# Last projection of a hybrid encoder layer: gate products one step ahead, and the merge's loads issued inside it

## The reference, cut to what matters

```python
xn = _rmsnorm(x, norm1_g)
z = xn @ w_in
u_x, u_g, q, k, v, f_logit, g_rnn, g_attn = jnp.split(z, SPLIT_POINTS, axis=-1)
...
rnn_y = (jax.nn.gelu(u_g) * h_seq.astype(x.dtype)) @ w_rnn_out
...
attn_y = attn.reshape(B, T, D_ATTN) @ w_attn_out
x = x + (jax.nn.sigmoid(g_rnn) * rnn_y + jax.nn.sigmoid(g_attn) * attn_y) @ w_o
x = x + _hier_moe(_rmsnorm(x, norm2_g), w_route_group, b_route_group, ...)
```

## Time and profile before

| | before |
|---|---|
| median of 3 runs | 2563.87 us |
| the profiled execution | 2562.86 us |
| its span | 2560.9 us |
| TensorE busy | 2178.7 us (85%) |
| VectorE busy | 1346.7 us (53%) |
| ScalarE busy | 1138.2 us (44%) |
| granted TensorE clock, mean | 0.932 |

### The profile page before, as it was taken

How to read it: one execution, slowest core, us unless ns; L and a number is a source line. 1 busy time by engine, 2 the same in 40 slices (tenths; PEclk the granted TensorE clock), 3 DMA queues, 4 the chain that set the end, 5 groups by cost and what they waited for, 6 DMA issues and landing times. The chain is left out here.

```text
span 2560.9 us, 36881 instructions
## 1 busy us (share of the span) xinstructions
PE 2178.7 (85%) x11116; PEld 1764.8 (69%) x11116; DVE 1346.7 (53%) x1576; ACT 1138.2 (44%) x1545; POOL 231.8 (9%) x299
## 2 busy tenths in 40 slices
PE   4469897988889897699999978995957999999993
PEld 2357675766767674599988868994845777777772
DVE  5423645455363545511155553213256888888886
ACT  3223444434344443321166543112224777777772
POOL 0210202112020200000000000000000100101013
PEclk9779999999999997799999998997978999999996
DMA  3310302111130201211122223104036999999997
GB/s 91 69 34 10 86 20 65 33 52 51 35 85 9 60 25 35 104 48 43 50 79 88 90 69 120 46 28 163 34 125 237 392 398 393 398 393 397 394 392 256
DMA packets 199087, 351.65 MB, mean 137 GB/s; under 512 B 19764, under 2 KB 127464, under 8 KB 198936
## 3 DMA queue, kind: packets, MB, share of 16 engines
q1 hardware_dynamic: 181560, 293.55, 32.1%
q0 software_dynamic: 13872, 44.74, 5.7%
q10 hardware_dynamic: 3584, 12.58, 1.2%
HBM read 301.87 MB, written 48.97 MB: 137 GB/s over the span
## 5 line engine op out<-in xcount | busy, mean ns | idle before, releaser
L2312 DVE TENSOR_TENSOR e_w_lo<-e_raw,e_w_hi 128x2048 fp32r<-128x2048 f32 x189 | 427.6, 2290 | 83.6 <-ACT e_w_hi L2242 65.2
L2242 ACT CAST e_w_hi<-e_raw 128x2048 fp32r<-128x2048 f32 x189 | 360.6, 1910 | 51.5 <-PE e_y_ps L103 33.7
L101 PE MATMUL proj_ps<-w_qkv_hi,xh 128*128 128x384 f32 x544 | 233.4, 429 | 24.8 <-PEq L287 19.1
L101 PE MATMUL ux_ps<-xh,r_wx_hi 128*128 128x364 f32 x576 | 191.4, 332 | 19.0 <-DVE r_wx_lo L768 15.5
L102 PE MATMUL ux_ps<-xl,r_wx_hi 128*128 128x364 f32 x576 | 190.5, 331 | 0.0
L103 PE MATMUL ux_ps<-xh,r_wx_lo 128*128 128x364 f32 x576 | 190.3, 330 | 0.0
L103 PE MATMUL proj_ps<-w_qkv_hi,xl 128*128 128x384 f32 x544 | 188.6, 347 | 0.0
L102 PE MATMUL proj_ps<-w_qkv_lo,xh 128*128 128x384 f32 x544 | 188.5, 346 | 0.0
L1188 PE MATMUL out_ps<-mT 128*128 128x512 f32 (+3 forms) x384 | 171.0, 528 | 2.9 <-DVEq L84 2.3
L101 PEld LDWEIGHTS proj_ps<-w_qkv_hi,xh 128*128 128x128 f32 x544 | 107.0, 197 | 51.3 <-issue 45.1
L1387 ACT ACTIVATE mT<-st_ps 128x512 f32<-128x512 f32 x192 | 93.9, 489 | 104.4 <-PE st_ps L1173 49.6
(11 more groups left out here) (425 smaller groups left out, 5107.9 us busy)
## 6 DMA issues: line engine op xcount, KB each, us to landing
e_raw<-w_gate_e SPq DMA_DIRECT2D x64, 1024.0 KB, 8.1
e_raw<-w_up_e SPq DMA_DIRECT2D x64, 1024.0 KB, 8.7
e_raw<-w_down_e SPq DMA_DIRECT2D x64, 1024.0 KB, 8.0
w_raw<-w_in SPq DMA_DIRECT2D x24, 512.0 KB, 4.4
r_wx<-w_in SPq DMA_DIRECT2D x24, 512.0 KB, 3.7
slot_y<-e_y ACTq DMA_DIRECT2D x32, 384.0 KB, 6.1
slot_y<-zrows POOLq DMA_DIRECT2D x24, 368.0 KB, 4.4
mT<-cache_k SPq DMA_DIRECT2D x8, 1024.0 KB, 5.5
```

The costliest lines, as they stand in the source:

```text
L101: nc.tensor.matmul(out, a_hi, b_hi, start=start, stop=False)
L2242: sc.copy(w_hi[u][:, :], w.raw[c][:, :]).then_inc(wh_ready, 1)
L2312: v.tensor_tensor(w_lo[u][:, :], w.raw[c][:, :], w_hi[u][:, :], ALU.subtract).then_inc(wl_ready, 1)
```

## The change

It has four parts.

1. `recurrent` ends with three steps more: SyncE loads the weights of gate 1, ScalarE takes gate 0's sigmoid (into a new tile `gate_sig` with two slots) and casts the weights, VectorE subtracts.
2. The last projection is a function of its own, `project_last`. TensorE's order is gate 1, projection 0, gate 2, projection 1, ..., gate 7, projection 6, projection 7. The sigmoid of gate c+1 goes to the slot that projection c doesn't use. Weights still pass through the one buffer `r_wx`, in the order projection 0, gate 2, projection 1, gate 3, ...
3. `w_o` is loaded as a whole, in four DMAs of 1 MB, over `xl`, and x over `xh`, as soon as gate 7's product has ended, by SyncE inside the projection's block. `merge` then casts and subtracts from there.
4. `turned_sb` of the merge has buffers of its own, and `got` of the expert stage lies over `mT`.

```diff
--- before.py
+++ after.py
@@ -455,6 +455,8 @@
                     load_bd(c + 1)
                 sp.wait_ge(x_split, KT)
                 sp.dma_start(w_x[:, :, :], g.w_in_k[:, :, COL_GATE_RNN:COL_GATE_RNN + P]).then_inc(g.gate_loaded, 16)
+                sp.wait_ge(g.gate_split, KT + 1)
+                sp.dma_start(w_x[:, :, :], g.w_in_k[:, :, COL_GATE_RNN + P:COL_GATE_RNN + 2 * P]).then_inc(g.gate_loaded, 16)
                 sp.wait_ge(tails_kept, 1)
...
@@ -571,6 +573,11 @@
                 with act.Fori(0, KT - 1) as c:
                     step(c, True)
                 step(KT - 1, False)
+                act.wait_ge(g.gate_ready, KT + 1)
+                nc.scalar.activation(g.sig[:, 0, :].rearrange("p (j t) -> p j t", t=THIRD), ux_ps[:, :, 0:THIRD], ACT.Sigmoid)\
+                    .then_inc(g.sig_ready, 1)
+                act.wait_ge(g.gate_loaded, KT * 16 + 32)
+                nc.scalar.copy(wx_split[0][:, :, :], w_x[:, :, :]).then_inc(g.gate_rounded, 1)
...
@@ -637,6 +644,8 @@
                     step(c, True)
                 step(KT - 1, False)
                 dve.sem_inc(tails_ready, 1)
+                dve.wait_ge(g.gate_rounded, KT + 2)
+                v.tensor_tensor(wx_split[1][:, :, :], w_x[:, :, :], wx_split[0][:, :, :], ALU.subtract).then_inc(g.gate_split, 1)
                 dve.wait_ge(tails_turned, 1)
                 edge(v.tensor_copy(tails_T[0:(2 * H + 2) * KT, :], ug_ps[0:(2 * H + 2) * KT, 0, 0:P]), tails_kept)
...
+def project_last(nc, g, sems, branch, w_out, gate_col):
...
+                load_p(0)
+                for k in range(KT):
+                    sp.dma_start(b_raw[:, k, :], branch[k]).then_inc(b_loaded[load_of(k)], 16)
+                with sp.Fori(0, KT - 2) as c:
+                    sp.wait_ge(p_split, before + c + 1)
+                    alone(sp, g)
+                    load_g(c + 2)
+                    sp.wait_ge(g_split, before + c + 3)
+                    alone(sp, g)
+                    load_p(c + 1)
+                sp.wait_ge(p_split, before + KT - 1)
+                load_p(KT - 1)
+                sp.wait_ge(gate_ready, before + KT)
+                for n in range(W_O_LOADS):
+                    ks = slice(n * KT // W_O_LOADS, (n + 1) * KT // W_O_LOADS)
+                    sp.dma_start(g.xn2[:, ks, :], g.w_o[0].rearrange("(k p) n -> p k n", p=P)[:, ks, :]).then_inc(g.wo_loaded[n], 16)
+                sp.dma_start(g.x1[:, 0:PT, :], g.x_prompt[0].rearrange("(t p) n -> p t n", p=P)).then_inc(g.x1_loaded, 16)
+                sp.dma_start(g.x1[0:T_SAMPLE, PT, :], g.x_sample[0]).then_inc(g.x1_loaded, 16)
...
+                with pe.Fori(0, KT - 1) as c:
+                    gate(c + 1)
+                    proj(c)
+                proj(KT - 1)
...
+                def squash(c, odd):
+                    act.wait_ge(gate_ready, before + c + 1)
+                    act.wait_ge(proj_taken, before + c)
+                    nc.scalar.activation(thirds(sig[:, odd, :]), gate_ps[:, :, 0:THIRD], ACT.Sigmoid).then_inc(sig_ready, 1)
+
+                def step(c, odd, more=True):
+                    act.wait_ge(proj_ready, before + c)
+                    round_p(c)
+                    squash(c + 1, 1 - odd)
+                    if more:
+                        round_g(c + 2)
+
+                squash(1, 1)
+                round_g(2)
+                with act.Fori(0, 2) as i:
+                    step(i * 2 + 1, 1)
+                    step(i * 2 + 2, 0)
+                step(5, 1)
+                step(6, 0, False)
+                act.wait_ge(proj_ready, before + KT - 1)
+                round_p(KT - 1)
...
+                def join(c, odd):
+                    chain = Chain(dve, chain_v, before + c * V_STEPS)
+                    dve.wait_ge(proj_ready, before + c + 1)
+                    dve.wait_ge(sig_ready, before + c + 2)
+                    m = g.mT[:, bass.ds(c, 1), 0:T_WIDE].rearrange("p o t -> p (o t)")
+                    chain(v.tensor_tensor(thirds(sig[:, odd, :]), thirds(sig[:, odd, :]), proj_ps[:, :, 0:THIRD], ALU.mult))
+                    chain(v.tensor_tensor(m, m, sig[:, odd, :], ALU.add), proj_taken)
+                    chain.ended(V_STEPS)
+
+                def step(c, odd, more=True):
+                    join(c - 1, 1 - odd)
+                    rest_p(c)
+                    if more:
+                        rest_g(c + 2)
+
...
+                rest_g(2)
+                with dve.Fori(0, 2) as i:
+                    step(i * 2 + 1, 1)
+                    step(i * 2 + 2, 0)
+                step(5, 1)
+                step(6, 0, False)
+                step(7, 1, False)
+                join(7, 1)
...
-        W_PARTS, K_EACH = KT, 1
-        w_raw = [sb(f"w_raw{b}", [P, K_EACH, D]) for b in range(2)]
+        w_raw = xn2
...
-        turned_sb = [raw[:, 0, :].rearrange("p (k t) -> p k t", k=KT) for raw in w_raw]
+        turned_sb = [sb(f"turned{b}", [P, KT, P]) for b in range(2)]
...
-                load_w(0)
-                load_w(1)
-                sp.dma_start(x1[:, 0:PT, :], g.x_prompt[0].rearrange("(t p) n -> p t n", p=P)).then_inc(x_loaded, 16)
-                sp.dma_start(x1[0:T_SAMPLE, PT, :], g.x_sample[0]).then_inc(x_loaded, 16)
...
-                for n in range(2, W_PARTS):
-                    sp.wait_ge(w_split, n - 1)
-                    load_w(n)
...
-                for n in range(W_PARTS):
-                    act.wait_ge(w_loaded[n % 2], 16 * (n // 2 + 1))
-                    sc.copy(w_o[0][:, ks_of(n), :], w_raw[n % 2][:, :, :]).then_inc(w_rounded, 1)
+                for k in range(KT):
+                    act.wait_ge(g.wo_loaded[k * W_O_LOADS // KT], 16)
+                    sc.copy(w_o[0][:, k, :], w_raw[:, k, :]).then_inc(w_rounded, 1)
...
-                for n in range(W_PARTS):
-                    dve.wait_ge(w_rounded, n + 1)
-                    v.tensor_tensor(w_o[1][:, ks_of(n), :], w_raw[n % 2][:, :, :], w_o[0][:, ks_of(n), :], ALU.subtract).then_inc(w_split, 1)
+                for k in range(KT):
+                    dve.wait_ge(w_rounded, k + 1)
+                    v.tensor_tensor(w_o[1][:, k, :], w_raw[:, k, :], w_o[0][:, k, :], ALU.subtract).then_inc(w_split, 1)
-                dve.wait_ge(x_loaded, 32)
+                dve.wait_ge(g.x1_loaded, 32)
...
-        got = [sb(f"got{t}", [P, D]) for t in range(NT)]
+        got_all = g.mT[:, :, :].rearrange("p k t -> p (k t)").rearrange("p (t n) -> p t n", n=D)
+        got = [got_all[:, t, :] for t in range(NT)]
...
-            with nc.sbuf_tensor("xn2", [P, NT, D], F32) as xn2:
-                merge(nc, g, x1, xn2, logits, tables)
...
+    g.mT = ctx.enter_context(nc.sbuf_tensor("mT", [P, KT, T_PAD], F32, side="right"))
+    rest = ExitStack()
+    g.xh = sb("xh", [P, KT, T_PAD], F32R)
+    x_end = nc.sbuf_base
+    g.xl = rest.enter_context(nc.sbuf_tensor("xl", [P, KT, T_PAD], F32R))
+    rest_end = nc.sbuf_base
+    assert KT * T_PAD == NT * D
+    g.x1, g.xn2 = (nc.alloc_sbuf_tensor_at(name, [P, NT, D], F32, offset=end - NT * D * 4) for name, end in (("x1", x_end), ("xn2", rest_end)))
+    g.wo_loaded, g.x1_loaded = [g.sem(f"wo_loaded{n}") for n in range(W_O_LOADS)], g.sem("x1_loaded")
...
-        project(nc, g, sems, 1, g.y_T, g.w_rnn_out, COL_GATE_RNN, True, "pr")
+        project_last(nc, g, sems, g.y_T, g.w_rnn_out, COL_GATE_RNN)
```

More of the change, by code:

```diff
@@ L2365, in _, with back @@
                                                x1[0:rows(t), t, :], ALU.mult, ALU.add).then_inc(summed, 1)
[L2368 removed]
+def back(nc, g, rest):
     with ExitStack() as ctx:
[L2371 to L2372 removed]
+        sb = lambda name, shape, dt=F32: ctx.enter_context(nc.sbuf_tensor(name, shape, dt, side="right"))
         gates, slots = sb("gates", [P, TOP_K, NT]), sb("slots", [P, TOP_K, NT], U32)
@@ L2375, in back @@
         tokens = sb("tokens", [CAP, BLOCKS_MAX + 2], U32)
-        with nc.sbuf_tensor("logits", [P, NT, GROUPS + EXPERTS], F32) as logits, ExitStack() as kept:
-            tables = RouteTables(nc, kept)
-            with nc.sbuf_tensor("xn2", [P, NT, D], F32) as xn2:
-                merge(nc, g, x1, xn2, logits, tables)
-            mixed.close()
-            with ExitStack() as weights:
-                w = ExpertWeights(nc, g, weights)
-                s = ExpertParts(nc, g, weights)
-                route(nc, g, w, s, tables, logits, gates, slots, passes, expert_of, tokens)
-                experts(nc, g, w, s, passes, expert_of, tokens, x1, gates, slots)
+        logits = sb("logits", [P, NT, GROUPS + EXPERTS])
+        tables = RouteTables(nc, ctx)
+        merge(nc, g, g.x1, g.xn2, logits, tables)
+        rest.close()
+        w = ExpertWeights(nc, g, ctx)
+        s = ExpertParts(nc, g, ctx)
+        route(nc, g, w, s, tables, logits, gates, slots, passes, expert_of, tokens)
+        experts(nc, g, w, s, passes, expert_of, tokens, g.x1, gates, slots)
```

(6 more changed lines are left out.)

102 lines of the change are left out of this document (82 added, 20 removed).

## The result

| | before | changed |
|---|---|---|
| median | 2562.94 us (4 runs, 2557.91 to 2565.27) | 2537.9 us (4 runs, 2537.37 to 2540.69) |
| the profiled execution | 2562.86 us | 2537.56 us |
| its span | 2560.9 us | 2535.7 us |
| granted clock, mean | 0.932 | 0.936 |

The ratio is 0.9902, 95% interval 0.9888 to 0.9915: 1.0% faster, inside the range and 1.6 us from the forecast. Of the 25.3 us between the two profiled executions I forecast 24.3. That the sum came so near is partly luck: it was 2.6 us short at the first edge and 1.0 at the second, and a loss of 2.6 us behind them made up for most of it.

What follows compares the result with a forecast made beforehand. The DMA-bound expert stage (635 us) stays untouched; idle TensorE edges at the last projection and merge can give time. Gains 2.2 + 22.1 = 24.3 us off the 2563.87 median give 2539.6, forecast 2539.5, range 2533 to 2547.

Steps and rivals of the forecast that it cites:

- first edge: Start of the last projection, where TensorE stood still 17.09 us: putting gate 1's product first gains 2.2 us.
- second edge: Start of the merge, where its first tile waited piece by piece for w_o: loading early gains 22.1 us.
- clock behind it costs: Projection 7, after the 4.2 us gap: TensorE at the lower clock, charged 2.6 us, bounds 0 and 2.6.
- T1: Start of the merge: 3.1 us behind projection 7's end at 1727.7, so at 1730.8.
- tile 0 done: Merge's first tile: ends at T1 + 17.1, bound by TensorE's clock, against T1 + 39.2 before.
- The tails: End of the recurrent stage: the tails' copy and four stores come 0.9 us later and delay SyncE by that; bounds 0 and 0.9.
- The order inside the loop: Last projection: thirteen products in a row from 1552.6, without waits, take 156.3 us and end at 1708.9.
- single weight buffer: Slower rival, last projection: loads through shared r_wx stall seven passes 5 us each, giving 2574 us; chance 0.01.
- cold start: Gate 1 at the last projection's start: half clock costs 2.6 us, so it takes 14.6 us.
- The new wait: Between projections 6 and 7: no gate product covers cast, multiply, add and subtraction, so TensorE waits 4.2 us.
- The loads: w_o and x, issued when gate 7 ends (1696.9), take 23.5 us, land by 1721 before the merge, without slowing TensorE.
- The clock-holds rival: Projection 7: the clock stays up over the gap before it, giving 2537 us; chance 0.2.

Runs made afterwards that it cites:

- spare banks: Against the changed kernel, projection 7's weights are rounded into the gate's dead halves and its product goes to the gate's dead PSUM banks; 2530.64 us, again 2529.51 us.
- filled gap: Changed kernel plus 22 matmuls whose results nobody uses between projections 6 and 7, the wait kept; 2539.98 us, ratio 0.9908 to the kernel before.
- loads only: Kernel before with its projection order kept, and w_o and x loaded early behind the last projection's loop; 2538.66 us, ratio 0.9897.
- the changed kernel's second: The changed kernel run once more, without edits, for a second profile; 2535.71 us, ratio 0.9894 to the kernel before.

## Why the prediction was right

Each step against the changed kernel's profile, in us:

| step | predicted | measured |
|---|---|---|
| gate 1 starts | 1538.0 | 1536.37 |
| gate 1 takes | 14.6 | 14.1 |
| projection 6 ends | 1708.9 | 1706.7 |
| new gap | 4.2 | 4.09 |
| clock behind it costs | 2.6 | 1.8 |
| T1 (ScalarE's first cast of the merge) | 1730.8 | 1728.16 |
| gain of the first edge (at T1) | 2.2 | 4.8 |
| tile 0 done | T1 + 17.1 | T1 + 16.8 (the add) |
| gain of the second edge | 22.1 | 23.05 |
| behind it | 0 | -2.6 |
| sum | 24.3 | 25.3 |

- *The tails.* This step failed. I had the later copy delay SyncE by 0.9 us. SyncE came 0.31 us earlier instead (1.2 us from my figure), and with the stores not waited for by SyncE at all the stage ended at the same place. I had taken the last store's issue and SyncE's next one as cause and effect because they stood next to each other in one queue; the store of y_T lies in another (POOL's), and I had not looked at it. The rule of the Trainium skill that I had set against my step ("DMA: Bandwidth & Descriptors", "Anatomy of one DMA": about 2 us of fixed time for a DMA, given there for one that GpSimd issues, while SyncE issues these) had the 0.9 vanish, and it did. That does not bear out the 2 us: no row shows these stores land, and the small loads of the merge took 3.4 to 3.7 us. TensorE followed SyncE by 0.39 us, not the 0.83 that I took from another stage's start.
- *The order inside the loop.* Right: no wait of TensorE from 1536.37 to 1706.7, thirteen products in 156.2 us (156.3 predicted). Neither the branch's split nor the single weight buffer stopped it. The price of the cold start was a bit lower, 2.1 us in place of 2.6 (gate 1 took 14.1).
- *The new wait.* Mechanism and length right, shown from both sides: the spare banks take it away (5.9 us), the filling keeps it and saves the clock. Only the clock's price was off. I took a whole cold start, 5.3 us at half rate; after 4.09 us the clock fell only once TensorE was 1.1 us into the product, and by 1715.3 it was up again, 3.4 us later. The Trainium skill ("TensorE: Matmul & The Clock Gate", "HAM oscillation — how this bites in real kernels") warns that gaps drop the clock; the trace agrees (4.09 us, then a PEclk of 0.50), and the filled gap shows the converse. It has the work behind such a gap start at the lower clock; here the first 1.1 us ran at the upper one.
- *The loads.* Right, and hidden as worked out (done at 1718, 1721 predicted). What I gave as one term of 22.1 us is two: about 13 from having all of `w_o` ahead of x and without the two-buffer ping-pong, about 9.5 from the earlier issue. That the burst costs TensorE nothing was right (the spare banks' last two joins are 11.96 us apart at over 400 GB/s), though I had read one of its numbers wrongly: the 2696 matmuls of the expert stage hold 392 small transposes beside the 2304 of 512 columns, so 0.216 us is no time of a 512-column matmul. With the transposes' 52 us taken out it is 0.230, the merge's 0.231.
- *The merge's start.* ScalarE began 2.20 us behind the start of VectorE's last add; before it was 1.71 us (1731.25 to 1732.96). This 0.5 I had not charged. It comes with `project_last`: all eleven profiles with it have about 2.2, and the loads only, which keep `project`, have 1.71 again. What in it costs the 0.5, no run here tells.
- *Behind the merge.* I changed nothing there, and 1.65 us went at the logits and 0.9 in the expert stage. The first is the clock, which in that place differs between executions, so it is not shown to be a cost of the change. The second is within what that stage differs by between executions (from the first expert load to the span's end: 672.9 us in the spare banks' second profile, 673.2 in the changed kernel's second and 674.2 in its first).

The clock-holds rival (2537) gave nearly the measured time for the wrong reason: the clock did not hold. The 2.6 us by which T1 came earlier than forecast are made up of smaller errors: 1.2 at SyncE's start, 0.4 from there to TensorE, 0.5 and 0.8 for the two stretches at half clock and 0.2 at the products and the gap, less the 0.5 at the merge's start.

## What to carry to other kernels

When a loop's neighbours are what hides a chain (here cast, join, subtraction behind each projection), look at the last pass, where the neighbour is missing: here its dead buffers were the cure, worth 5.9 us. Before charging a delay at a stage's end, list every queue's last transfer, not only the one in which the stage's next instruction stands. Small loads that are wanted soon go ahead of large ones or wait for them to be over: 3.7 us against 13.8 for the same 128 KB.
